# Low halves of the last weight tiles moved from VectorE to GpSimd, and three gathered-row dots a lot instead of one, in the routing stage of a hybrid block

## The chip, the cores and the metric

One Trainium2 chip, one core. The metric is device time in microseconds (us) of one execution of the whole program, the median of several runs. Three runs of the kernel before took 2127.27, 2131.42 and 2134.3 us.

## The reference, cut to what matters

A streaming encoder block: projection, sparse attention and a linear recurrence, a gated join with layer norm, and then PEER, a retrieval of single-neuron experts. The change lies in PEER alone. `eb` is the expert chosen (128 picks a token), `gb` its gate:

```python
def _peer(x, wq, subkeys, u, v):
    q = (xf @ wq).reshape(n, PEER_HEADS, 2, PEER_HALF)
    s = jnp.einsum('nhpd,hpkd->nhpk', q, subkeys)
    s_top, i_top = lax.top_k(s, PEER_TOPK)                 # 16 of 128, two sides
    cand = s_top[:, :, 0, :, None] + s_top[:, :, 1, None, :]
    best_s, best_j = lax.top_k(cand.reshape(n, PEER_HEADS, -1), PEER_TOPK)
    ...
    h = jnp.einsum('nd,nhkd->nhk', xb, u[eb])              # one dot a pick
    coef = gb * jax.nn.gelu(h, approximate=False)
    return jnp.einsum('nhk,nhkd->nd', coef, v[eb])
```

There are 16384 experts of width 1024 and 512 tokens. All of it is float32.

## The kernel before, in words

The program runs in stages, with a barrier of all engines between them: projection, attention, scan, join, then `route` (L1536) and `experts` (L1974).

**Two ways to reach the experts.** Tokens 128 to 511 (384 of them) are done densely: every expert's hidden value is computed and multiplied by a gate that is zero for experts not picked. Tokens 0 to 127 are done by gathering: GpSimd (POOL) issues an indirect DMA (`gather_rows`, L1944) that brings one picked row of `u`, later of `v`, for each of the 128 tokens, 512 KB at a time, into one of 8 slots. VectorE takes the dot of the rows with the tokens (`dot_rows`, L1956, one custom instruction over 128x1024 and a short read of the accumulator) or adds the scaled rows to the sum (`add_rows`, L1965). There are 128 dots and then 128 adds. The first `GATHERED_EARLY` = 24 dots are done in `route`, the rest in `experts`.

**float32 products.** A product is made of three passes: high by high, low part of the tokens by high of the weight, and low of the weight by high of the tokens. ScalarE (ACT) copies a weight tile of 128x1024 to its high part (`high`, L1660, `w_hl[..., 0, :]`), and another engine subtracts it from the staged tile, which gives the low part (`low`). TensorE does 16 matmuls with the high part (L1739), waits for the low part, and does 8 more (L1743).

**The route stage.** A stream of weight tiles passes through a ring of four (SP loads, ACT makes the high part, somebody the low part, TensorE multiplies). 56 tiles come first (six a head, and 8 in between), and their low parts are made by GpSimd (L1640) while VectorE ranks the scores (L1822 to L1886). Then come 24 *lots* (`LOTS`). A lot makes the dense gates of 16 tokens, from one-hot matrices, and has two tiles of the stream (2 x 24 = 48):

- VectorE: `four` (L1912) four times a lot. Each makes the one-hot matrices of four tokens by two comparisons of 128x512 (L1918, L1920) and one product of 128x1024 (L1922). Before the first lot, in the middle of each and at the end of each but the last, it makes the low part of a tile (`low`, L1926 to L1929, 48 in all), and after each lot one dot of a gathered row (L1941).
- TensorE: tile, two fours (L1796), tile, two fours.
- ACT: the high parts, the gelu of each tile's product, its store ("parked"), and the copies of the fours' sums to the lot (L1712).
- SP: the load of tile s + 4 once the low part of s is made, and the store of the lot.
- POOL: after the 56 low parts it issues the 24 gathers. From the ninth on each waits until its slot has been used.

VectorE may run four fours ahead of TensorE (L1917), no more. `RING` is also 4, so the high part of a tile waits for the product four tiles before it.

**The experts stage.** 128 steps k. For each, `v` tile k is loaded, split in high (ACT) and low (VectorE, L2179), the hidden values are weighed with the gates (L2170) and split (L2085, L2174), and TensorE adds 18 matmuls of 512 columns (L2135). The hidden values of the first 88 (`PARKED`) come from DRAM; the last 40 are computed here (L2121, L2125), with the low part of their `u` tile by VectorE (L2158). A table `used_by` says how many gathered rows VectorE has taken by the end of each step: one a step in the first 88, and the rest spread evenly over the 37 after them:

```python
used_by = [GATHERED_EARLY + (k + 1 if k < PARKED else
           min(PARKED + (2 * PICKS - GATHERED_EARLY - PARKED) * (k + 1 - PARKED) // (FRESH - 3),
               2 * PICKS - GATHERED_EARLY))
           for k in range(EXPERT_KEYS)]
```

After the last step come the layer norm and the stores.

Of the kernel before, what the change touches and what calls it, by code (L numbers as in the profile page):

```python
# [18 lines left out]
F32 = mybir.dt.float32  # L19
# [3 lines left out]
ALU = mybir.AluOpType  # L23
# [23 lines left out]
LOTS = DENSE // LOT  # L47
BETWEEN = 8
PARKED = 4 * PEER_HEADS + BETWEEN + 2 * LOTS
GATHER_RING, GATHERED_EARLY = 8, 24  # L50
MARK, FILL, LOW = -3.4e38, -3.3e38, -1.0e30


# [1482 lines left out]
def route(nc, a, g):  # L1536

    ps, ident, h1T, h_hl, dense, parked = g["ps"], g["ident"], g["h1T"], g["h_hl"], g["dense"], g["parked"]
    h_tok, gathering = g["h_tok"], g["gathering"]
# [4 lines left out]
    TILES_A_LOT = 2  # L1544
# [6 lines left out]
    RING = 4  # L1551
    with ExitStack() as ctx:
# [33 lines left out]
        rows_landed, rows_order = sem("rows_landed"), sem("rows_order")  # L1586
        landed = [sem(f"w_landed{j}") for j in range(RING)]
        h_high, h_low = sem("h_high"), sem("h_low")
        w_high, w_low, late_low = sem("w_high"), sem("w_low"), sem("late_low")
        tile_done, gelu_made = sem("tile_done"), sem("gelu_made")  # L1590
        act_parked = [sem(f"act_parked{j}") for j in range(2)]
        keys_landed, counted = sem("sub_keys_landed"), sem("counted")
# [5 lines left out]
        hot_ready, four_done, four_copied = sem("hot_ready"), sem("four_done"), sem("four_copied")  # L1598
        lot_stored = [sem(f"lot_stored{j}") for j in range(2)]
        block = ctx.enter_context(nc.Block())  # L1600
        BY_POOL = FIRST_LOT
        tile_bank = lambda n, is_query: n % 2 if is_query else 2 + n % 2

        def expert_of(s):
# [3 lines left out]
        @block.sync  # L1608
        def _(sp):
            def load(s, j):  # L1610
                sp.dma_start(staged[:, j % RING, :], a["stream"][s]).then_inc(landed[j % RING], 16)

            for j in range(RING):
                load(j, j)
            sp.dma_start(g_row, a["ln1_g"].partition_broadcast(P)).then_inc(rows_landed, 16)
            sp.dma_start(b_row, a["ln1_b"].partition_broadcast(P)).then_inc(rows_landed, 16)
            sp.dma_start(sub_keys[:, :, :], a["sub_keys"]).then_inc(keys_landed, 16)
            with sp.Fori(0, BY_POOL // 8) as i:
                for j in range(8):
                    sp.wait_ge(w_low, i * 8 + (j + 1))  # L1620
                    load(i * 8 + (j + RING), j)
            for n in range(LOTS):
                for s in range(FIRST_LOT + TILES_A_LOT * n, FIRST_LOT + TILES_A_LOT * (n + 1)):
                    if s + RING < STREAMED:
                        sp.wait_ge(late_low, s - BY_POOL + 1)
                        load(s + RING, s)
                sp.wait_ge(four_copied, 4 * (n + 1))
                sp.dma_start(dense[n], lot[:, n % 2, :, :].rearrange("p k n -> p (k n)")).then_inc(lot_stored[n % 2], 16)
            for j in range(2):
                sp.wait_ge(lot_stored[j], 16 * (LOTS // 2))  # L1630
                sp.wait_ge(act_parked[j], 16 * (PARKED // 2 + 1))

        @block.gpsimd
        def _(pool):
            nc.gpsimd.iota(count16[:, :], [[1, K]], 0, 0, allow_small_or_imprecise_dtypes=True).then_inc(counted, 1)
            nc.gpsimd.iota(count128[:, :], [[1, P]], 0, 0, allow_small_or_imprecise_dtypes=True).then_inc(counted, 1)

            def low(s, j):
                pool.wait_ge(w_high, s + 1)
                nc.gpsimd.tensor_tensor(w_hl[:, j % RING, 1, :], staged[:, j % RING, :],  # L1640
                                        w_hl[:, j % RING, 0, :].bitcast(F32), ALU.subtract).then_inc(w_low, 1)

            with pool.Fori(0, BY_POOL // 8) as i:
                for j in range(8):
                    low(i * 8 + j, j)
            pool.wait_ge(gathering["picked"], 1)
            for n in range(GATHERED_EARLY):
                gather_rows(nc, pool, a, gathering, n)

        @block.scalar  # L1650
        def _(act):
# [75 lines left out]
        @block.tensor  # L1727
        def _(pe):
            pe.sem_inc(tile_done, 1)

            def tile(s, j, m, is_query, before, low):

                pe.wait_ge(w_high, s + 1)
                pe.wait_ge(*before)
                lo, hi = (0, SEQ) if is_query else (SEQ - DENSE, SEQ)
                bank = ps[:, tile_bank(m, is_query), 0:hi - lo]
                for k in range(KD):
                    for part in range(2):
                        nc.tensor.matmul(bank, w_hl[:, j % RING, 0, P * k:P * (k + 1)], h_hl[:, part, k, lo:hi],  # L1739
                                         start=(k == 0 and part == 0), stop=False)  # L1740
                pe.wait_ge(*low)
                for k in range(KD):
                    last = nc.tensor.matmul(bank, w_hl[:, j % RING, 1, P * k:P * (k + 1)], h_hl[:, 0, k, lo:hi],  # L1743
                                            start=False, stop=(k == KD - 1))
                last.then_inc(tile_done, 1)

            def scores(i, r):
                pe.wait_ge(keys_landed, 16)
                for x in range(2):
                    pe.wait_ge(q_copied, i * 4 + (2 * r + x + 3))  # L1750
                    pe.wait_ge(s_copied, i * 4 + (2 * r + x + 1))
                    for t in range(NT):
                        last = nc.tensor.matmul(ps[:, 4 + 2 * r + x, P * t:P * (t + 1)], qT[:, x, P * t:P * (t + 1)],
                                                sub_keys[:, i * 4 + (2 * r + x), :], start=True, stop=True)
                    last.then_inc(s_done, 1)

            pe.wait_ge(h_high, KD)
            pe.wait_ge(h_low, KD)

            with pe.Fori(0, PEER_HEADS // 2) as i:  # L1760
                for j in range(2 * PER_HEAD):
                    r, m = j // PER_HEAD, j % PER_HEAD
                    s = i * (2 * PER_HEAD) + j
                    if m < 2:
                        tile(s, j, m, True, (q_copied, i * 4 + (2 * r + m + 1)), (w_low, s + 1))
                        continue
                    if m == 3:
                        scores(i, r)
                    n = 4 * r + m - 2
                    tile(s, j, n, False, (gelu_made, i * 8 + (n + 1)), (w_low, s + 1))  # L1770

            def expert(s):
                n = expert_of(s)
                tile(s, s, n, False, (gelu_made, n + 1),
                     (w_low, s + 1) if s < BY_POOL else (late_low, s - BY_POOL + 1))

            for j in range(BETWEEN):
                if j == GATES_AT:
                    pe.wait_ge(s_copied, QUERIES + 4)
                    pe.wait_ge(gates_ready, 1)  # L1780
                    for x in range(3):
                        for t in range(1, NT):
                            last = nc.tensor.transpose(ps[:, 4 + x, P * (t - 1):P * t], picks[:, x, t, :], ident[:, :])
                        last.then_inc(picks_turned, 1)
                expert(TOPK_TILES + j)
            pe.wait_ge(picks_copied, 3)

            def four(u):

                q = u % 4  # L1790
                if u >= 4:
                    pe.wait_ge(four_copied, u - 3)
                pe.wait_ge(hot_ready, u + 1)
                for n in range(FOUR):
                    for part in range(2):
                        last = nc.tensor.matmul(ps[:, 4 + q, P * n:P * (n + 1)], hot2[:, q, n, :],  # L1796
                                                hot1_hl[:, q, part, n, :], start=(part == 0), stop=(part == 1))
                last.then_inc(four_done, 1)

            for n in range(LOTS):  # L1800
                for half in range(2):
                    expert(FIRST_LOT + TILES_A_LOT * n + half)
                    four(4 * n + 2 * half)
                    four(4 * n + 2 * half + 1)

        @block.vector
        def _(dve):
# [115 lines left out]
                                 gate_hl[:, :, now].bitcast(F32).unsqueeze(3).broadcast_to([P, 2, FOUR, P]), ALU.mult  # L1923
                                 ).then_inc(hot_ready, 1)

            def low(s):  # L1926
                dve.wait_ge(w_high, s + 1)
                v_.tensor_tensor(w_hl[:, s % RING, 1, :], staged[:, s % RING, :],  # L1928
                                 w_hl[:, s % RING, 0, :].bitcast(F32), ALU.subtract).then_inc(late_low, 1)  # L1929

            low(BY_POOL)
            for n in range(LOTS):
                four(4 * n)
                four(4 * n + 1)
                low(BY_POOL + TILES_A_LOT * n + 1)
                four(4 * n + 2)
                four(4 * n + 3)
                if n + 1 < LOTS:
                    low(BY_POOL + TILES_A_LOT * (n + 1))
                if n < GATHERED_EARLY:  # L1940
                    dot_rows(nc, dve, h_tok, gathering, n)  # L1941


def gather_rows(nc, pool, a, gathering, n):  # L1944
# [347 lines left out]
```

## Time and profile before

| | before |
|---|---|
| median of 3 runs | 2131.42 us |
| lowest, highest | 2127.27, 2134.3 us |
| the profiled execution, its own time | 2135.26 us |
| its span in the trace | 2133.5 us |
| TensorE / VectorE / ACT / GpSimd busy | 1929.4 / 1608.0 / 757.5 / 567.8 us |
| route, from its first instruction to the last lot's store | 758.3 to 1379.5 us |
| of it the 24 lots on VectorE | 1071.4 to 1378.1 us |
| experts | 1384.5 us to the end |

In the rows below PE is TensorE, PEld its weight loads, DVE VectorE, ACT ScalarE, POOL GpSimd, SP SyncE; a trailing q is an engine's queue. A row of a group of instructions gives busy time, mean of one, and the idle time before it. DVE instructions overlap a little at their ends, so that the step from one start to the next (for instance 1.14 us) is shorter than the duration written (1.22 us). Idle time of an engine that is not the bottleneck costs nothing.

### The profile page before, as it was taken

Reading aid. Unit: us, or ns where it says so; the run is one execution under the profiler, and the core shown is the slowest. Engines: PE = TensorE matmul, PEld = TensorE weight load, DVE = VectorE, ACT = ScalarE, POOL = GpSimd, SP = SyncE. Lnnn points to the kernel's source line nnn. Section 1 sums busy time; section 2 is a strip of 40 time slices with the busy share of each in tenths; the row PEclk is TensorE's granted clock in tenths of the full one; section 3 lists DMA queues with packets and bytes.
Section 4 is the critical chain, followed back from the end, with each engine's and each line's share of the span. In section 5 each row is a group of like instructions: output and inputs, shape, how many; then the busy total and the mean of one; then the engine's idle time right before and its main releaser. Section 6 shows DMA issues by size and latency. Waiting matters only on the chain. (4 is left out here: it accounts for less than half of the span.)

```text
span 2133.5 us, 33188 instructions
## 1 busy us (share of the span) xinstructions
PE 1929.4 (90%) x12866; PEld 1648.7 (77%) x12866; DVE 1608.0 (75%) x2830; ACT 757.5 (36%) x1114; POOL 567.8 (27%) x395
## 2 busy tenths in 40 slices
PE   5989998889998979999499999849999999999996
PEld 4878875359863469999499999738888888999995
DVE  6288993314545279999699999848888888899998
ACT  3222554432220043333145555423333333333332
POOL 2322442000000044555200000022222224566660
PEclk9989998778999989999799999969999999999998
DMA  3211231010041054444366676399999998999992
GB/s 121 79 50 60 90 118 40 1 41 3 4 159 40 0 177 128 133 135 144 110 217 234 231 242 209 146 342 343 361 355 343 362 350 305 375 388 379 380 402 107
DMA packets 169683, 410.97 MB, mean 193 GB/s; under 512 B 13504, under 2 KB 85184, under 8 KB 166352
## 3 DMA queue, kind: packets, MB, share of 16 engines
q1 hardware_dynamic: 117712, 253.41, 34.8%
q0 software_dynamic: 36864, 134.23, 16.7%
q10 hardware_dynamic: 14976, 21.50, 2.8%
q8 instruction: 92, 1.51, 0.3%
q14 instruction: 39, 0.32, 0.0%
HBM read 360.33 MB, written 48.76 MB: 192 GB/s over the span
## 5 line engine op out<-in xcount | busy, mean ns | idle before, releaser
L2135 PE MATMUL ps<-v_hl,coef_hl 128*128 128x512 f32 x2304 | 535.6, 392 | 40.1 <-DVE coef_hl L2174 40.1
L2135 PEld LDWEIGHTS ps<-v_hl,coef_hl 128*128 128x128 f32 x2304 | 434.6, 189 | 130.7 <-DVE coef_hl L2174 41.5
L1739 PE MATMUL ps<-h_hl,w_hl 128*128 128x384 f32 (+1 forms) x1664 | 329.0, 350 | 8.8 <-DVE h_hl L1811 8.8
L1739 PEld LDWEIGHTS ps<-h_hl,w_hl 128*128 128x128 f32 x1664 | 295.8, 191 | 20.1 <-issue 9.2
L1951 POOL DMA_INDIRECT gathered_rows<-in_u_rows,pick_index x128 | 134.8, 1053 | 612.6 <-DVE pick_hidden L1961 499.9
L2079 ACT ACTIVATE v_hl<-v_staged 128x1024 fp32r<-128x1024 f32 x128 | 135.3, 1057 | 260.6 <-PE ps L2135 193.4
L2179 DVE TENSOR_TENSOR v_hl<-v_staged,v_hl 128x1024 fp32r<-128x1024 f32 x128 | 156.6, 1223 | 68.8 <-ACT v_hl L2079 68.0
L1951 POOL DMA_INDIRECT gathered_rows<-in_v,pick_index x128 | 176.2, 1377 | 104.9 <-DVE h_tok L1970 74.1
L1640 POOL TENSOR_TENSOR w_hl<-w_staged,w_hl 128x1024 fp32r<-128x1024 f32 x56 | 143.1, 2558 | 152.7 <-ACT w_hl L1665 152.4
L1970 DVE SCALAR_TENSOR_TENSOR h_tok<-gathered_rows,pick_hidden,h_tok 128x1024 f32<-128x1024 f32 x128 | 164.2, 1283 | 10.1
L1743 PE MATMUL ps<-h_hl,w_hl 128*128 128x384 f32 (+1 forms) x832 | 168.0, 343 | 0.7 <-DVE w_hl L1928 0.7
L633 PE MATMUL ps<-hT_hl,w_hl 128*128 128x264 f32 (+1 forms) x1024 | 167.9, 322 | 0.0
L633 PEld LDWEIGHTS ps<-hT_hl,w_hl 128*128 128x128 f32 x1024 | 150.4, 198 | 14.4 <-issue 2.8
L298 POOL TENSOR_TENSOR w_hl<-w_staged,w_hl 128x1024 fp32r<-128x1024 f32 x40 | 102.8, 2572 | 211.9 <-ACT w_hl L481 211.9
L1961 DVE CUSTOM_DVE_ANT_0 gathered_rows<-gathered_rows,h_tok 128x1024 f32<-128x1024 f32 x128 | 155.2, 1219 | 0.0
L1743 PEld LDWEIGHTS ps<-h_hl,w_hl 128*128 128x128 f32 x832 | 147.4, 188 | 6.0 <-DVE w_hl L1928 1.0
L2085 ACT ACTIVATE coef_hl<-coef 128x384 fp32r<-128x384 f32 x128 | 65.7, 513 | 160.8 <-DVE coef L2170 160.8
L1665 ACT ACTIVATE w_hl<-w_staged 128x1024 fp32r<-128x1024 f32 x104 | 110.5, 1064 | 24.0 <-ACT h1T L1671 16.0
L2121 PE MATMUL ps<-h_hl,u_hl 128*128 128x384 f32 x640 | 118.4, 336 | 0.0
L1922 DVE TENSOR_TENSOR hot_hl<-h1T,gate_hl 128x1024 fp32r<-128x1024 f32 x96 | 117.2, 1220 | 0.0
L2121 PEld LDWEIGHTS ps<-h_hl,u_hl 128*128 128x128 f32 x640 | 113.1, 188 | 3.1
L1712 ACT ACTIVATE lot<-ps 128x512 f32<-128x512 f32 x96 | 99.7, 1099 | 35.2 <-PE ps L1796 35.0
(319 smaller groups left out, 2791.1 us busy)
## 6 DMA issues: line engine op xcount, KB each, us to landing
v_staged<-in_v SPq DMA_DIRECT2D x128, 512.0 KB
w_staged<-in_stream SPq DMA_DIRECT2D x104, 512.0 KB
dense_gates<-lot SPq DMA_DIRECT2D x24, 1024.0 KB, 4.8
gates<-dense_gates SPq DMA_DIRECT2D x16, 1536.0 KB
w_staged<-in_w_in_t SPq DMA_DIRECT2D x40, 512.0 KB
h1T<-in_stream SPq DMA_DIRECT2D x40, 512.0 KB
parked_gelu<-h1T ACTq DMA_DIRECT2D x88, 192.0 KB
coef<-parked_gelu SPq DMA_DIRECT2D x88, 192.0 KB
```

Of the source, the lines that this page charges most:

```text
L633: nc.tensor.matmul(banks[b], w_hl[:, j, 0, P * k:P * (k + 1)], hT_hl[:, part, k, lo:hi], start=(k == 0 and part == 0), stop=False)
L1640: nc.gpsimd.tensor_tensor(w_hl[:, j % RING, 1, :], staged[:, j % RING, :], w_hl[:, j % RING, 0, :].bitcast(F32), ALU.subtract).then_inc(w_ ...
L1739: nc.tensor.matmul(bank, w_hl[:, j % RING, 0, P * k:P * (k + 1)], h_hl[:, part, k, lo:hi], start=(k == 0 and part == 0), stop=False)
L1743: last = nc.tensor.matmul(bank, w_hl[:, j % RING, 1, P * k:P * (k + 1)], h_hl[:, 0, k, lo:hi], start=False, stop=(k == KD - 1))
L1922: v_.tensor_tensor(hot1_hl[:, r], is_key[:, u % 2].unsqueeze(1).broadcast_to([P, 2, FOUR, P]), gate_hl[:, :, now].bitcast(F32).unsqueeze(3 ...
L1951: nc.gpsimd.indirect_dma_start(gathering["rows"][:, slot, :], None, table, bass.IndirectOffsetOnAxis(gathering["index"][:, column:column + ...
L1961: nc.vector.tensor_tensor_reduce(rows, rows, h_tok[:, 0, :], 1.0, 0.0, ALU.mult, ALU.add, gathering["hidden"][:, n:n + 1]).then_inc(gather ...
L1970: nc.vector.scalar_tensor_tensor(h_tok[:, 0, :], gathering["rows"][:, slot, :], gathering["hidden"][:, pick:pick + 1], h_tok[:, 0, :], ALU ...
L2079: nc.scalar.activation(v_hl[:, k % HLS, 0, :], v_staged[:, k % STAGED, :], ACT.Copy).then_inc(v_high, 1)
L2121: nc.tensor.matmul(bank, u_hl[:, f % 2, 0, P * c:P * (c + 1)], h_hl[:, part, c, SEQ - DENSE:SEQ], start=(c == 0 and part == 0), stop=False)
L2135: last = nc.tensor.matmul(ps[:, 2 + 2 * t + half, :], coef_hl[:, k % HLS, c, P * t:P * (t + 1)], v_hl[:, k % HLS, v, 512 * half:512 * (hal ...
L2179: v_.tensor_tensor(v_hl[:, k % HLS, 1, :], v_staged[:, k % STAGED, :], v_hl[:, k % HLS, 0, :].bitcast(F32), ALU.subtract).then_inc(v_low, 1)
```

## The change

GpSimd makes the low parts of all 104 tiles of the route stage, in its own order of work: after the 56 it issues six gathers, and then for each lot it makes two low parts and issues up to three gathers. VectorE makes none. It does three dots a lot instead of one, one in the middle and two after the fours. `GATHERED_EARLY` goes from 24 to 72, which also changes `used_by`. One semaphore counts all low parts.

```diff
--- before.py
+++ after.py
@@ -47,7 +47,8 @@
 LOTS = DENSE // LOT
 BETWEEN = 8
 PARKED = 4 * PEER_HEADS + BETWEEN + 2 * LOTS
-GATHER_RING, GATHERED_EARLY = 8, 24
+GATHER_RING, DOTS_A_LOT = 8, 3
+GATHERED_EARLY = DOTS_A_LOT * LOTS
 MARK, FILL, LOW = -3.4e38, -3.3e38, -1.0e30
 
 
@@ -1586,7 +1587,7 @@
         rows_landed, rows_order = sem("rows_landed"), sem("rows_order")
         landed = [sem(f"w_landed{j}") for j in range(RING)]
         h_high, h_low = sem("h_high"), sem("h_low")
-        w_high, w_low, late_low = sem("w_high"), sem("w_low"), sem("late_low")
+        w_high, w_low = sem("w_high"), sem("w_low")
         tile_done, gelu_made = sem("tile_done"), sem("gelu_made")
         act_parked = [sem(f"act_parked{j}") for j in range(2)]
         keys_landed, counted = sem("sub_keys_landed"), sem("counted")
@@ -1598,7 +1599,6 @@
         hot_ready, four_done, four_copied = sem("hot_ready"), sem("four_done"), sem("four_copied")
         lot_stored = [sem(f"lot_stored{j}") for j in range(2)]
         block = ctx.enter_context(nc.Block())
-        BY_POOL = FIRST_LOT
         tile_bank = lambda n, is_query: n % 2 if is_query else 2 + n % 2
 
         def expert_of(s):
@@ -1615,14 +1615,14 @@
             sp.dma_start(g_row, a["ln1_g"].partition_broadcast(P)).then_inc(rows_landed, 16)
             sp.dma_start(b_row, a["ln1_b"].partition_broadcast(P)).then_inc(rows_landed, 16)
             sp.dma_start(sub_keys[:, :, :], a["sub_keys"]).then_inc(keys_landed, 16)
-            with sp.Fori(0, BY_POOL // 8) as i:
+            with sp.Fori(0, FIRST_LOT // 8) as i:
                 for j in range(8):
                     sp.wait_ge(w_low, i * 8 + (j + 1))
                     load(i * 8 + (j + RING), j)
             for n in range(LOTS):
                 for s in range(FIRST_LOT + TILES_A_LOT * n, FIRST_LOT + TILES_A_LOT * (n + 1)):
                     if s + RING < STREAMED:
-                        sp.wait_ge(late_low, s - BY_POOL + 1)
+                        sp.wait_ge(w_low, s + 1)
                         load(s + RING, s)
                 sp.wait_ge(four_copied, 4 * (n + 1))
                 sp.dma_start(dense[n], lot[:, n % 2, :, :].rearrange("p k n -> p (k n)")).then_inc(lot_stored[n % 2], 16)
@@ -1640,12 +1640,17 @@
                 nc.gpsimd.tensor_tensor(w_hl[:, j % RING, 1, :], staged[:, j % RING, :],
                                         w_hl[:, j % RING, 0, :].bitcast(F32), ALU.subtract).then_inc(w_low, 1)
 
-            with pool.Fori(0, BY_POOL // 8) as i:
+            with pool.Fori(0, FIRST_LOT // 8) as i:
                 for j in range(8):
                     low(i * 8 + j, j)
             pool.wait_ge(gathering["picked"], 1)
-            for n in range(GATHERED_EARLY):
+            for n in range(2 * DOTS_A_LOT):
                 gather_rows(nc, pool, a, gathering, n)
+            for n in range(LOTS):
+                for s in range(FIRST_LOT + TILES_A_LOT * n, FIRST_LOT + TILES_A_LOT * (n + 1)):
+                    low(s, s)
+                for x in range(DOTS_A_LOT * (n + 2), min(DOTS_A_LOT * (n + 3), GATHERED_EARLY)):
+                    gather_rows(nc, pool, a, gathering, x)
 
         @block.scalar
         def _(act):
@@ -1771,8 +1776,7 @@
 
             def expert(s):
                 n = expert_of(s)
-                tile(s, s, n, False, (gelu_made, n + 1),
-                     (w_low, s + 1) if s < BY_POOL else (late_low, s - BY_POOL + 1))
+                tile(s, s, n, False, (gelu_made, n + 1), (w_low, s + 1))
 
             for j in range(BETWEEN):
                 if j == GATES_AT:
@@ -1923,22 +1927,14 @@
                                  gate_hl[:, :, now].bitcast(F32).unsqueeze(3).broadcast_to([P, 2, FOUR, P]), ALU.mult
                                  ).then_inc(hot_ready, 1)
 
-            def low(s):
-                dve.wait_ge(w_high, s + 1)
-                v_.tensor_tensor(w_hl[:, s % RING, 1, :], staged[:, s % RING, :],
-                                 w_hl[:, s % RING, 0, :].bitcast(F32), ALU.subtract).then_inc(late_low, 1)
-
-            low(BY_POOL)
             for n in range(LOTS):
                 four(4 * n)
                 four(4 * n + 1)
-                low(BY_POOL + TILES_A_LOT * n + 1)
+                dot_rows(nc, dve, h_tok, gathering, DOTS_A_LOT * n)
                 four(4 * n + 2)
                 four(4 * n + 3)
-                if n + 1 < LOTS:
-                    low(BY_POOL + TILES_A_LOT * (n + 1))
-                if n < GATHERED_EARLY:
-                    dot_rows(nc, dve, h_tok, gathering, n)
+                for x in range(DOTS_A_LOT * n + 1, DOTS_A_LOT * (n + 1)):
+                    dot_rows(nc, dve, h_tok, gathering, x)
 
 
 def gather_rows(nc, pool, a, gathering, n):
```

## Rows read from the trace of the kernel before

**Rows 1.** The page: busy time of the engines, and the span in 40 slices
```profile
PE 1929.4 (90%) x12866; PEld 1648.7 (77%) x12866; DVE 1608.0 (75%) x2830; ACT 757.5 (36%) x1114; POOL 567.8 (27%) x395
...
DVE  6288993314545279999699999848888888899998
```

**Rows 2.** Busy time by stretch: lots, parked steps, fresh steps, two stretches of other stages
```profile
core 0: us, PE busy (x) PEld busy (x) DVE busy (x) ACT busy (x) POOL busy (x), PEclk, DMA share, GB/s
1072.00:1377.00 305.00, 289.11 (x1894) 286.41 (x1895) 305.00 (x383) 160.98 (x186) 18.33 (x16) 0.99 0.62 213
1440.00:1760.00 320.00, 320.00 (x1413) 265.05 (x1413) 259.44 (x392) 115.70 (x158) 79.26 (x79) 1.00 1.00 352
1774.00:2097.00 323.00, 323.00 (x1635) 294.09 (x1635) 299.92 (x310) 107.55 (x152) 189.37 (x137) 1.00 0.96 359
684.00:701.20 17.20, 11.87 (x25) 4.94 (x24) 5.80 (x3) 0.00 (x0) 0.00 (x0) 0.80 0.00 0
460.40:477.60 17.20, 13.16 (x249) 10.59 (x248) 5.49 (x28) 5.62 (x17) 0.00 (x0) 0.68 0.35 126
```

**Rows 3.** Instructions in order of time, one lot and the start of the next
```profile
1200.29 0.68 DVE L1918 TENSOR_TENSOR h1T<-count,picksT 128x512 f32<-128x512 f32 x1
1200.63 1.15 POOL L1951 DMA_INDIRECT gathered_rows<-in_u_rows,pick_index  x1 [11.63 <-DVE pick_hidden L1961]
...
1201.49 1.22 DVE L1922 TENSOR_TENSOR hot_hl<-h1T,gate_hl 128x1024 fp32r<-128x1024 f32 x1
...
1202.63 0.68 DVE L1918 TENSOR_TENSOR h1T<-count,picksT 128x512 f32<-128x512 f32 x1
...
1211.92 1.22 DVE L1961 CUSTOM_DVE_ANT_0 gathered_rows<-gathered_rows,h_tok 128x1024 f32<-128x1024 f32 x1
...
1213.06 0.69 DVE L1918 TENSOR_TENSOR h1T<-count,picksT 128x512 f32<-128x512 f32 x1
```

**Rows 4.** Groups of instructions (busy, mean ns, idle before), the lots (1072 to 1377 us)
```profile
L1928 DVE TENSOR_TENSOR w_hl<-w_staged,w_hl 128x1024 fp32r<-128x1024 f32 x48 | 58.6, 1220 | 0.0
```

**Rows 5.** Instructions in order of time, VectorE's first work in the lots and its last four
```profile
1071.39 1.23 DVE L1928 TENSOR_TENSOR w_hl<-w_staged,w_hl 128x1024 fp32r<-128x1024 f32 x1
...
1375.72 1.23 DVE L1922 TENSOR_TENSOR hot_hl<-h1T,gate_hl 128x1024 fp32r<-128x1024 f32 x1
```

**Rows 6.** Lines L1818 (VectorE) and L1640 (GpSimd): duration ns min/median/max, first and last start
```profile
L1818 DVE TENSOR_TENSOR h_tok<-h_tok,gathered_rows x8: 1212/2306/3419, 768.8 to 785.7; 128x1024 f32<-128x1024 f32 x8
...
L1640 POOL TENSOR_TENSOR w_hl<-w_staged,w_hl x56: 2339/2402/3384, 764.0 to 1052.1; 128x1024 fp32r<-128x1024 f32 x56
```

**Rows 7.** Instructions in order of time, where GpSimd's low parts meet VectorE's work
```profile
1004.06 4.55 DVE L1873 TENSOR_TENSOR is_place<-place,count 128x1024 f32<-128x1024 f32 x2
...
1005.04 2.49 POOL L1640 TENSOR_TENSOR w_hl<-w_staged,w_hl 128x1024 fp32r<-128x1024 f32 x1 [1.84 <-ACT w_hl L1665]
...
1044.02 0.69 DVE L1894 TENSOR_TENSOR picks<-picks,small 128x512 f32<-128x512 f32 x1
...
1046.40 2.34 POOL L1640 TENSOR_TENSOR w_hl<-w_staged,w_hl 128x1024 fp32r<-128x1024 f32 x1 [34.26 <-ACT w_hl L1665]
...
1046.52 2.77 DVE L1900 TENSOR_TENSOR picks<-picks,small 128x512 f32<-128x512 f32 x1
```

**Rows 8.** GpSimd before the lots: its first and its third gather
```profile
1054.61 1.12 POOL L1951 DMA_INDIRECT gathered_rows<-in_u_rows,pick_index  x1 [0.17 <-issue]
...
1057.28 0.94 POOL L1951 DMA_INDIRECT gathered_rows<-in_u_rows,pick_index  x1 [0.30 <-issue]
```

**Rows 9.** First products of the first and of the last fresh step on TensorE
```profile
1773.47 0.87 PE L2121 MATMUL ps<-h_hl,u_hl 128*128 128x384 f32 x4
...
2097.43 0.87 PE L2121 MATMUL ps<-h_hl,u_hl 128*128 128x384 f32 x4
```

**Rows 10.** Instructions in order of time after the last fresh product
```profile
2103.05 1.23 PEld L2135 LDWEIGHTS ps<-v_hl,coef_hl 128*128 128x128 f32 x6 [0.32 <-DVE coef_hl L2174]
...
2105.12 9.43 PEld L2135 LDWEIGHTS ps<-v_hl,coef_hl 128*128 128x128 f32 x42 [0.84 <-DVE coef_hl L2174]
```

## The prediction

> **What bounds the kernel now.** I read the busy line and the slices first. TensorE is busy for 90% of the span, and VectorE stands at 9 tenths in slices 21 to 25, which are the lots [rows 1]. The share of the whole says little here, so I took one stretch of each part that the change touches [rows 2]. In the lots VectorE is busy 305.00 us of 305.00 and TensorE 289.11: VectorE is the bound, and TensorE is close behind. In the parked and the fresh steps of the experts stage TensorE is busy 320.00 of 320.00 and 323.00 of 323.00, and VectorE has room (259.44 and 299.92). So what VectorE does in the lots is on the path that sets the end, and what it does in the experts stage is beside it.
>
> In order of time a lot reads as follows [rows 3]. A four goes from 1200.29 (two comparisons) over 1201.49 (its product) to the next four at 1202.63, which is 1.20 + 1.14 = 2.34 us. The dot steps from 1211.92 to the next comparison at 1213.06: 1.14 us. The low part is of the same size; its mean duration is 1220 ns [rows 4], against 1.22 of the dot, and I take the same 1.14 us step. The lot is then 4 x 2.34 + 2 x 1.14 + 1.14 = 12.78 us, and the rows say 1213.06 - 1200.29 = 12.77. VectorE has no gap at all.
>
> **The change, part by part.** VectorE's own work first. Two low parts a lot (2.28 us) go and two dots (2.28 us) come: nothing, lot for lot. At the two ends something is left. From the first low part at 1071.39 to the end of the last product of a four, 1375.72 + 1.23 = 1376.95 [rows 5], VectorE did 96 fours, 48 low parts and 23 dots (the last dot comes after). Now it does 96 fours and 70 dots (three in each of 23 lots and one in the last; two follow the last four). 71 instructions become 70: -1.1 us. So by count alone the lots gain a microsecond. The 48 dots taken from the experts stage are the only gain left, and there they are beside TensorE.
>
> How much that is worth: the first product of the first fresh step is at 1773.47, that of the last at 2097.43, and there are 39 steps between [rows 9]. 323.96 / 39 = 8.31 us a step, with TensorE full all the way. Fewer rows a step (96 over 37 steps, 2.6, in place of 144, 3.9) free VectorE, not TensorE: 0. In the parked steps there is one row a step before and after, so they stay as they are. The gelu and the change from dots to adds move from a fresh to a parked step; VectorE has 60 us of room over 320 there, and three buffers stand between it and TensorE: 0, and up to 3 us if the buffers do not cover it. At the very end TensorE waits for VectorE's last low parts of the coefficients, 0.32 + 0.84 us [rows 10]. A VectorE that is not behind takes these away: -1.2 us, between 0 and -2.
>
> **Now what GpSimd brings.** Its low part takes 2339 to 3384 ns, median 2402 [rows 6], twice VectorE's. Two of these and three issues of gathers at about 1.15 us [rows 3] are 2 x 2.40 + 3 x 1.15 = 8.3 us of a lot of 12.78, so GpSimd has the time. The question is what VectorE does meanwhile. Line L1818 is a product or sum of two tiles in SBUF, 128x1024 on VectorE, as the low part is. It takes 1212 ns at least and 3419 ns at most, within 17 us in which GpSimd makes low parts [rows 6]. The excess is 3419 - 1212 = 2.21 us, about the duration of one GpSimd low part. GpSimd's own longest is longer by about 1 us, a VectorE instruction. The two take turns. It holds for operands that are repeated, as those of the comparisons are: two of L1873 take 4.55 us with one GpSimd low part begun 0.98 us into them [rows 7], against 2 x 1.14 + 0.08 = 2.36 without, so 2.19 us more. It holds for 128x512: L1900 takes 2.77 us with GpSimd's 1046.40 beside it, L1894 of the same shape 0.69 [rows 7], so 2.08 us more. In the lots before, GpSimd only issued gathers, and nothing of this was to be seen.
>
> The Trainium skill says the same in other words, and it speaks against the change: by "SBUF — State Buffer", section "Who interferes with whom", a VectorE instruction with two inputs in SBUF and a GpSimd instruction that reads SBUF share an interface, and the second to issue is blocked until the first is done. By that rule alone the dots would be held up as well, which no row of before shows; the trace agrees with it for products, sums and comparisons.
>
> Where the low parts of the lots fall. After the 56 low parts GpSimd's first gather starts at 1054.61 and its third at 1057.28 [rows 8], 1.34 us for each; six of them and two low parts end at about 1054.6 + 8.0 + 4.8 = 1067.4, before VectorE's lots begin at 1071.39 [rows 5]. These two cost nothing. From then on the third gather of a lot waits for the dot in the middle of the lot before it, because of the ring of eight, and the two low parts of the next lot stand behind that gather on GpSimd's queue. They begin some 1.6 us after the middle dot (0.3 to the issue, 1.15 for it), so both meet the third and fourth four, whose nine or so microseconds are all comparisons and products; no dot and no gap covers them. They end some 5 us before TensorE's next tile asks for them, and SP's loads, which wait for the low parts, leave no later than before. So 46 low parts (48 less 2) hold VectorE for their time: 46 x 2.2 = 101 us. Bounds: 46 x 2.08 = 96 (L1900) and 46 x 2.40 = 110 (the whole median of GpSimd's instruction). I take 2.2, from L1818, since its row is a steady stream as the lots are.
>
> Sum: -1.1 + 101 + 0 - 1.2 = +99 us (92 to 112). A lot goes from 12.8 to 17.2 us. TensorE's need is 289.11 / 24 = 12.0 us a lot, so it waits some 5 us in each. DMA: two more gathers of 512 KB a lot, but 4.4 us more time for them; at 213 GB/s before [rows 2] that is about 3.7 MB in 17.2 us, much the same rate.
>
> **The profiled execution** took 2135.26 us, 3.8 above the median 2131.42. 2135.3 + 99 = 2234, and on the scale of the median 2131.4 + 99 = 2230.
>
> **The rivals.**
>
> *TensorE's clock makes it the bound.* With 5 us of idle in 17.2, most of it in one gap before the fourth four, the granted clock may fall. Stretches of this length with TensorE busy 11.87 and 13.16 us were granted 0.80 and 0.68 [rows 2]. TensorE becomes the bound below 12.0 / 17.2 = 0.70. Against it: an engine that is late has no gaps, and in the lots of before, with hardly any gap, it was 0.99. If it takes 18.3 us a lot: 24 x 1.1 = 26 more, 2256.
>
> *Part of the low parts is covered.* If the pieces of a four with repeated operands let GpSimd in, or GpSimd slides under the dots at the end of the lot (2.3 us of the 4.4) and these do not take turns with it, up to half is saved: -50, 2180; with a quarter, 2205. Against: L1873, and the place in the order worked out above.
>
> *No turns are taken in the lots* (the other side: not slower). Place: the comparisons and products of L1918 to L1922 against L1640. If these forms do not meet GpSimd, nothing of the 101 us remains and -1.1 - 1.2 gives 2129. It decides as soon as a low part costs VectorE less than 2.3 / 46 = 0.05 us. For it speaks only that these very lines were never seen beside a GpSimd low part. This is also the case in which the change does nothing at all.
>
> **How the numbers follow.** Turns are taken at full price: 0.80, 2230, its own range 2222 to 2243. TensorE's clock: 0.07. Partly covered: 0.07. Not slower: 0.06. The range reaches from a quarter covered to the case of the clock, 2203 to 2256. A measurement of this kernel can tell about 0.3% (6.4 us) from no change. Faster by more than that needs a gain that I can't find in any row: 0.01. The same: 0.05. Slower: 0.94.
>
> **What would show it.** Right: the three lines of a four with maxima 2.2 us above their present 0.69 and 1.22, in pairs in the third and fourth four of a lot; their sum of busy time higher by some 100 us; GpSimd's low parts at 2.4 to 3.4 us; a lot of 17.2 us, with TensorE idle in it by some 5 us, put down to hot_hl; fresh steps still at 8.31 us. Wrong: a lot of 12.8 us (no turns), or one of over 18 us with TensorE full at a lower clock, or dots longer than 1.22 us, which would say that the low parts lie elsewhere than I put them.

## The result and the profile after

The changed kernel takes 2244.11 us, the median of 4 runs (2242.41 to 2253.25), against 2131.32 before (4 runs too): a ratio of 1.0539, interval 1.0506 to 1.0573, or 113 us more. The profiled execution took 2244.01 us over a span of 2242.3.

The page, with the same lines as [rows 1], and the busy time by stretch that answers to the first three stretches of [rows 2] (lots, parked steps, fresh steps):

```profile
PE 1977.2 (88%) x12866; PEld 1692.8 (75%) x12866; DVE 1669.0 (74%) x2782; ACT 759.1 (34%) x1114; POOL 682.6 (30%) x443
...
DVE  5388973134452599996999999956888877778776
```
```profile
1072.00:1480.00 408.00, 332.32 (x1842) 322.52 (x1842) 408.00 (x415) 159.65 (x182) 189.68 (x110) 0.87 0.60 218
1555.00:1875.00 320.00, 320.00 (x1413) 264.96 (x1413) 259.75 (x364) 115.99 (x157) 84.80 (x78) 1.00 1.00 352
1884.00:2206.00 322.00, 322.00 (x1629) 293.11 (x1629) 251.02 (x251) 108.25 (x155) 120.35 (x89) 1.00 0.82 283
```

VectorE is busy throughout the lots, as before (408.00 of 408.00 us), but they are 114 us longer. In the fresh steps it has 71 us of room where it had 23, and TensorE is full there as before: the dots moved out of that stage bought nothing.

VectorE's groups in the lots, 1072 to 1480 us (busy, mean ns, idle before), and below them the instructions of VectorE and GpSimd in order of time in half a lot:

```profile
L1926 DVE TENSOR_TENSOR hot_hl<-h1T,gate_hl 128x1024 fp32r<-128x1024 f32 x92 | 223.0, 2424 | 0.0
L1957 DVE CUSTOM_DVE_ANT_0 gathered_rows<-gathered_rows,h_tok 128x1024 f32<-128x1024 f32 x70 | 83.4, 1215 | 0.0
L1922 DVE TENSOR_TENSOR h1T<-count,picksT 128x512 f32<-128x512 f32 x92 | 64.8, 705 | 0.0
L1924 DVE TENSOR_TENSOR hot<-count,picksT 128x512 fp32r<-128x512 f32 x92 | 62.6, 680 | 0.0
```
```profile
1214.95 0.68 DVE L1922 TENSOR_TENSOR h1T<-count,picksT 128x512 f32<-128x512 f32 x1
...
1215.55 0.68 DVE L1924 TENSOR_TENSOR hot<-count,picksT 128x512 fp32r<-128x512 f32 x1
...
1216.15 6.15 DVE L1926 TENSOR_TENSOR hot_hl<-h1T,gate_hl 128x1024 fp32r<-128x1024 f32 x1
1216.46 4.75 POOL L1640 TENSOR_TENSOR w_hl<-w_staged,w_hl 128x1024 fp32r<-128x1024 f32 x2
```

The product of a four has a mean of 2424 ns; before, the lines of a four had no instruction over 1.23 us [rows 3, 5]. The excess is not spread over them. One product a lot, the first behind the middle dot, takes 6.15 us, and inside it lie both of GpSimd's low parts. 21 of the 96 products are like this (mean 6131 ns), one took 8414 with three low parts inside, and all others 1.2 us. In the whole stage L1922 had one at 2881 ns. No dot was held.

From the first comparison of the lots to the end of the last product it is 304.4 us before and 418.5 after: +114.0. The rest of the 108.8 us between the two spans is small: the stages ahead of `route`, which the change does not touch, ended 4.4 us earlier in this execution; the low part ahead of the first four is gone (-1.0); up to the first sum -0.1; the parked steps +0.7; the 40 fresh steps 0.0; the end -0.3. From the first comparison to the end of the span it is 1061.0 us before and 1175.2 after, 114.2 more, so nothing behind the lots gave any of it back.

### The profile page after: what moved, and what is told of

The parts are those of the page before. It is cut to its first block and busy times, and to the rows that moved or that the text cites. A ratio compares the mean times of both kernels' runs of the same rounds, so it can differ in the third digit from the quotient of the medians.

```text
span 2242.3 us, 33187 instructions
## 1 busy us (share of the span) xinstructions
PE 1977.2 (88%) x12866; PEld 1692.8 (75%) x12866; DVE 1669.0 (74%) x2782; ACT 759.1 (34%) x1114; POOL 682.6 (30%) x443
## 5 line engine op out<-in xcount | busy, mean ns | idle before, releaser
L1744 PE MATMUL ps<-h_hl,w_hl 128*128 128x384 f32 (+1 forms) x1664 | 359.5, 373 | 8.7 <-DVE h_hl L1815 8.7
L1744 PEld LDWEIGHTS ps<-h_hl,w_hl 128*128 128x128 f32 x1664 | 326.8, 210 | 20.1 <-issue 9.1
L1640 POOL TENSOR_TENSOR w_hl<-w_staged,w_hl 128x1024 fp32r<-128x1024 f32 x104 | 256.8, 2483 | 160.9 <-ACT w_hl L1670 160.1
L1947 POOL DMA_INDIRECT gathered_rows<-in_u_rows,pick_index x128 | 144.1, 1126 | 404.7 <-DVE pick_hidden L1957 364.8
L1947 POOL DMA_INDIRECT gathered_rows<-in_v,pick_index x128 | 168.0, 1312 | 282.6 <-DVE h_tok L1966 241.0
L1926 DVE TENSOR_TENSOR hot_hl<-h1T,gate_hl 128x1024 fp32r<-128x1024 f32 x96 | 227.9, 2374 | 0.0
L1800 PE MATMUL ps<-hot_hl,hot 128*128 128x128 f32 x768 | 114.1, 302 | 77.4 <-DVE hot_hl L1926 77.4
L1800 PEld LDWEIGHTS ps<-hot_hl,hot 128*128 128x128 f32 x768 | 107.8, 217 | 87.7 <-issue 60.4
L1748 PE MATMUL ps<-h_hl,w_hl 128*128 128x384 f32 (+1 forms) x832 | 168.0, 343 | 0.0
L299 POOL TENSOR_TENSOR w_hl<-w_staged,w_hl 128x1024 fp32r<-128x1024 f32 x40 | 102.9, 2572 | 211.8 <-ACT w_hl L482 211.8
L1748 PEld LDWEIGHTS ps<-h_hl,w_hl 128*128 128x128 f32 x832 | 147.9, 188 | 5.0
L1717 ACT ACTIVATE lot<-ps 128x512 f32<-128x512 f32 x96 | 99.7, 1081 | 117.0 <-PE ps L1800 117.0
L2166 DVE TENSOR_TENSOR coef<-coef,gates 128x384 f32<-128x384 f32 x128 | 71.1, 555 | 78.1 <-ACT coef L2086 56.2
## 6 DMA issues: line engine op xcount, KB each, us to landing
gates<-dense_gates SPq DMA_DIRECT2D x16, 1536.0 KB, 13.8
```

The costliest lines, as they stand in the source:

```text
L1926: v_.tensor_tensor(hot1_hl[:, r], is_key[:, u % 2].unsqueeze(1).broadcast_to([P, 2, FOUR, P]), gate_hl[:, :, now].bitcast(F32).unsqueeze(3 ...
L1947: nc.gpsimd.indirect_dma_start(gathering["rows"][:, slot, :], None, table, bass.IndirectOffsetOnAxis(gathering["index"][:, column:column + ...
```

## The experiments

Each time is a median of two to ten runs, set against the kernel before, run again at the same time (2127.9 to 2129.4 us). The ratios are those on record over all runs and can differ from the quotient of the two medians in the fourth digit. "The lots" is the stretch from the first comparison to the end of the last product, in the profiled execution. The price of a low part is what the lots take above VectorE's own count, divided by 46. The count is 2.341 us for each of the 96 fours and 1.144 us for each dot ahead of the last product, which are the steps where nothing meets them.

**Only the low parts moved.**

```diff
-GATHER_RING, DOTS_A_LOT = 8, 3
+GATHER_RING, DOTS_A_LOT = 8, 1
```

> The changed kernel with one dot a lot instead of three: of the change only the low parts are moved. Theory (GpSimd and VectorE take turns at their SBUF inputs): VectorE's own work is 12.8 - 2.3 = 10.5 us a lot, and the two low parts of GpSimd hold it for 2 x 2.2 to 2 x 2.45 us more, as in the changed kernel, where 21 products took 6.13 us in place of 1.22. A lot is 14.9 to 15.4 us, the lots from the first comparison to the last product 304 + 23 x (2.1 to 2.6) = 353 to 364 us, the whole 2180 to 2192 us. Rival (the two further gathers of a lot are what costs, through GpSimd's queue or the DMA engines): VectorE is free of low parts and TensorE is the bound with 12.0 us a lot, and the whole is 2115 to 2125 us.

2177.5 us against 2128.8 (ratio 1.0231, 1.0197 to 1.0264): a little below the band of the theory, and far from the rival. The lots took 350.8 us. VectorE's count is 96 x 2.341 + 23 x 1.144 = 251.0, so 99.7 / 46 = 2.17 us a low part. Three dots are among the instructions held (3.39 to 3.40 us). VectorE and GpSimd here, in order of time:

```profile
1204.64 1.21 DVE L1926 TENSOR_TENSOR hot_hl<-h1T,gate_hl 128x1024 fp32r<-128x1024 f32 x1
1205.77 1.21 DVE L1957 CUSTOM_DVE_ANT_0 gathered_rows<-gathered_rows,h_tok 128x1024 f32<-128x1024 f32 x1
...
1206.91 2.86 DVE L1922 TENSOR_TENSOR h1T<-count,picksT 128x512 f32<-128x512 f32 x1
```
```profile
1204.44 4.79 POOL L1640 TENSOR_TENSOR w_hl<-w_staged,w_hl 128x1024 fp32r<-128x1024 f32 x1 [5.56 <-ACT w_hl L1670]
```

GpSimd's low part starts at 1204.44, within a comparison, and lets a product and a dot pass that began after it; then the next comparison is held, 2.86 us in place of 0.68. 11 of the 46 low parts were passed in this way. The low parts come as ScalarE's high parts come, one at a time, and what VectorE has next is held.

**Only the dots moved.** The kernel before, with the low parts by VectorE:

```diff
-GATHER_RING, GATHERED_EARLY = 8, 24
+GATHER_RING, DOTS_A_LOT = 8, 3
+GATHERED_EARLY = DOTS_A_LOT * LOTS
...
                 low(BY_POOL + TILES_A_LOT * n + 1)
+                dot_rows(nc, dve, h_tok, gathering, DOTS_A_LOT * n)
...
-                if n < GATHERED_EARLY:
-                    dot_rows(nc, dve, h_tok, gathering, n)
+                for x in range(DOTS_A_LOT * n + 1, DOTS_A_LOT * (n + 1)):
+                    dot_rows(nc, dve, h_tok, gathering, x)
```

> The kernel before with three dots a lot and 72 early gathers, the low parts still made by VectorE: of the change only the dots are moved. Theory: nothing but their count costs, 47 dots before the last product x 1.14 = 54 us more in the lots (15.1 us a lot), the product at 1.22 us throughout, and nothing back in the experts stage, whose fresh steps stay at 8.31 us: 2131 + 54 = 2185 us, 2181 to 2190. Rival (taking gathers out of the experts stage frees something there): a few to 10 us less than that, with fresh steps under 8.31 us. With the run that moves only the low parts, the two should add up to the 113 us of the change.

2178.6 us (1.0236, 1.0203 to 1.0269), 50 us more in the median and 2 us below the band. The lots took 358.7, which is 54.3 more, as counted (47 x 1.144 = 53.8), with no instruction of VectorE over 1.25 us in them. From the first comparison to the end of the span it is 1115.0 us against 1061.0, so the 54 us are there in full; what is missing lies ahead of the lots, where the edit changes nothing (the first comparison is at 1061.5 here and at 1072.5 before). The fresh steps stayed at 8.31 us: from 1816.69 to 2140.65 over 39. So nothing came back, and the rival is out. Low parts alone (+46.4 in the lots) and dots alone (+54.3) make 100.7 of the 114.0. The 13.3 that are left are in the price of a low part: 2.17 us with the low parts alone, (418.5 - 304.8) / 46 = 2.47 in the changed kernel, and 46 x 0.30 = 13.8.

**Does the dot take turns as well?** The three dots together in the middle, and the low parts released by the first of them:

```diff
+            for s in range(FIRST_LOT, FIRST_LOT + TILES_A_LOT):
+                low(s, s)
             for n in range(LOTS):
-                for s in range(FIRST_LOT + TILES_A_LOT * n, FIRST_LOT + TILES_A_LOT * (n + 1)):
+                pool.wait_ge(gathering["used"], DOTS_A_LOT * n + 1)
+                for s in range(FIRST_LOT + TILES_A_LOT * (n + 1), min(FIRST_LOT + TILES_A_LOT * (n + 2), STREAMED)):
+                    low(s, s)
...
-                dot_rows(nc, dve, h_tok, gathering, DOTS_A_LOT * n)
+                for x in range(DOTS_A_LOT * n, DOTS_A_LOT * (n + 1)):
+                    dot_rows(nc, dve, h_tok, gathering, x)
                 four(4 * n + 2)
                 four(4 * n + 3)
-                for x in range(DOTS_A_LOT * n + 1, DOTS_A_LOT * (n + 1)):
-                    dot_rows(nc, dve, h_tok, gathering, x)
```

> The changed kernel with the three dots of a lot together in its middle, and GpSimd's two low parts of the next lot released by the first of them, ahead of its gathers, so that the low parts begin some 0.3 us into the second dot. Theory A (the dot, a custom instruction with two SBUF inputs, takes turns too): a dot of about 6 us in place of the long product, a lot stays at 17.7 us and the whole at 2235 to 2250 us. Theory B (the dot does not meet GpSimd): dots stay at 1.22 us, some 2 us of each lot's 4.8 us of low parts run beneath them, the instruction after them is held for the rest (about 3 us), a lot is 15.5 to 16.2 us and the whole 2190 to 2210 us.

2232.7 us (1.0490, 1.0457 to 1.0524), 2 us below the range of theory A and 23 above that of theory B. In order of time:

```profile
1207.81 1.22 DVE L1959 CUSTOM_DVE_ANT_0 gathered_rows<-gathered_rows,h_tok 128x1024 f32<-128x1024 f32 x1
1207.96 6.62 POOL L1640 TENSOR_TENSOR w_hl<-w_staged,w_hl 128x1024 fp32r<-128x1024 f32 x2 [6.22 <-DVE pick_hidden L1959]
...
1208.95 3.38 DVE L1959 CUSTOM_DVE_ANT_0 gathered_rows<-gathered_rows,h_tok 128x1024 f32<-128x1024 f32 x1
...
1212.26 2.87 DVE L1925 TENSOR_TENSOR h1T<-count,picksT 128x512 f32<-128x512 f32 x1
```

The dot is held too: 23 dots have a mean of 3396 ns. Theory B is out. But theory A's six-microsecond dot is not there either. The engines alternate: GpSimd waits for the dot that runs (two low parts take 6.62 us in place of 4.75), the next dot waits for GpSimd, the second low part for that dot, the comparison for the second low part. The price is (408.5 - 307.1) / 46 = 2.20 us. The Trainium skill's "SBUF — State Buffer", section "Who interferes with whom", says that a VectorE instruction with two inputs in SBUF contends with a GpSimd instruction that reads SBUF. The dot has two such inputs, and at 3396 ns in place of 1218 the trace agrees.

**One input out of SBUF.** The same work as the changed kernel, with the counting row and the gates copied once to two free banks of PSUM:

```diff
...
+            count_ps, gate_ps = ps[:, 0, DENSE:DENSE + P], ps[:, 0:2, 0:DENSE]
+            v_.tensor_copy(count_ps, count128[:, :]).then_inc(in_psum, 1)
+            v_.tensor_copy(gate_ps, gate_hl[:, :, :].bitcast(F32)).then_inc(in_psum, 1)
+            dve.wait_ge(in_psum, 2)
...
-                count = count128[:, :].unsqueeze(1).broadcast_to([P, FOUR, P])
+                count = count_ps.unsqueeze(1).broadcast_to([P, FOUR, P])
...
-                                 gate_hl[:, :, now].bitcast(F32).unsqueeze(3).broadcast_to([P, 2, FOUR, P]), ALU.mult
+                                 gate_ps[:, :, now].unsqueeze(3).broadcast_to([P, 2, FOUR, P]), ALU.mult
```

> The changed kernel with one operand of each instruction of a four in PSUM (the counting row for both comparisons, the gates for the product, in two banks that are free by then): same work, one SBUF input instead of two. Theory (it is the second SBUF input that meets GpSimd's reads): the products stay near 1.22 us or what an operand in PSUM makes of them, GpSimd's low parts take 2.34 to 2.4 us, a lot is 12.8 us and the whole 2126 to 2135 us. If PSUM makes an instruction slower by 0.1 us, 12 x 24 x 0.1 = 29 us more. Rival (any VectorE instruction, or its writes, meets GpSimd): 2240 to 2250 us as before.

2163.4 us (1.0164, 1.0133 to 1.0195): 81 us less than the changed kernel, and 28 above the upper end of what the theory gave. Lines of the product and of the dot (duration ns min/median/max), and a piece in order of time:

```profile
L1930 DVE TENSOR_TENSOR hot_hl<-h1T,ps x96: 1201/1206/1219, 1071.7 to 1405.4; 128x1024 fp32r<-128x1024 f32 x96
```
```profile
L1961 DVE CUSTOM_DVE_ANT_0 gathered_rows<-gathered_rows,h_tok x128: 1207/1218/4833, 1075.2 to 1672.5; 128x1024 f32<-128x1024 f32 x128
```
```profile
1203.76 4.74 POOL L1640 TENSOR_TENSOR w_hl<-w_staged,w_hl 128x1024 fp32r<-128x1024 f32 x2
```
```profile
1205.98 1.21 DVE L1930 TENSOR_TENSOR hot_hl<-h1T,ps 128x1024 fp32r<-128x1024 f32 x1
1207.11 2.49 DVE L1961 CUSTOM_DVE_ANT_0 gathered_rows<-gathered_rows,h_tok 128x1024 f32<-128x1024 f32 x1
```

44 products in which a low part began took 1207 ns. Their output is in SBUF as before, so it is the second input that meets GpSimd, not the write. What is left is the dots, whose inputs are still both in SBUF: the low parts end at 1208.50, the fours at 1207.11, so 21 dots stand at about 2.5 us, one at 3.4 and one at 4.8. All 72 took 119.9 us instead of 87.5, which is 32 us. A slower operand in PSUM, which the expectation had priced at 29 us, would have given nearly the same total, but no instruction of a four was slower: the longest product took 1219 ns, the longest comparison 693.

**The dot out of the low parts' way.** The same with the middle dot ahead of all four fours of a lot:

```diff
+                dot_rows(nc, dve, h_tok, gathering, DOTS_A_LOT * n)
                 four(4 * n)
                 four(4 * n + 1)
-                dot_rows(nc, dve, h_tok, gathering, DOTS_A_LOT * n)
```

> The run with one operand of the fours in PSUM and three dots a lot took 34 us more than the kernel before, and in it 22 dots of 72 stood at 2.5 us: the low parts began 1.3 us after the middle dot and ran 4.8 us, past the two fours that follow (4.7 us), into a dot. Here the middle dot stands ahead of all four fours, so that the low parts have 9.3 us of fours to run beside. Theory (only the dots meet GpSimd now): no dot over 1.3 us, lots 305 us, the whole 2126 to 2134 us, the same as before the change, with three dots a lot and all low parts made by GpSimd. Rival (something else of the three dots costs, such as 295 GB/s of loads in the lots): 2150 to 2165 us.

2126.9 us (0.9999, 0.9985 to 1.0013): no difference from before. The dot's line now says

```profile
L1961 DVE CUSTOM_DVE_ANT_0 gathered_rows<-gathered_rows,h_tok x128: 1212/1216/1225, 1063.1 to 1632.2; 128x1024 f32<-128x1024 f32 x128
```

and the lots took 302.5 us, with the same two more gathers a lot. With the meetings gone, the change costs nothing, and gains nothing, as its count of instructions said. The rival is out.

**The operand in PSUM by itself,** in the kernel before (same edit):

> The kernel before, with nothing changed but one operand of each instruction of a four in PSUM. In the last run the product took 1206 ns in place of 1219 and the comparisons 0.68 us as ever. So the operand in PSUM is worth nothing by itself: 2126 to 2134 us, no difference that can be told. If it were worth more (over 6 us), the gain of the run with one dot would not be GpSimd's.

2130.7 us against 2129.4 (1.0001, 0.9982 to 1.0021): no difference that can be told.

**One input in PSUM and one dot a lot,** the low parts by GpSimd: the edit with PSUM above, and `DOTS_A_LOT` from 3 to 1:

> As the run with one operand of each instruction of a four in PSUM, but with one dot a lot, as before the change: GpSimd makes the low parts, VectorE has only the fours (which no longer meet them) and one dot. Theory: VectorE needs 4 x 2.34 + 1.14 = 10.5 us a lot, and at most one dot a lot is held, by 1.3 to 2.2 us; TensorE needs 12.0 us a lot and becomes the bound, so that the lots last about 24 x 12.1 = 290 us against 304 before, and the whole takes 2113 to 2122 us. Rival (the lots stay bound by something else, such as ScalarE's copies or the loads behind the low parts): 2127 to 2135 us, no gain.

2113.8 us against 2129.4 (0.9917, 0.9892 to 0.9942), 16 us or 0.8% faster than before, within the band of the theory. The lots took 280.6 us against 304.4. Busy time by stretch in the lots:

```profile
1072.00:1355.00 283.00, 281.78 (x1874) 281.64 (x1874) 276.14 (x332) 158.40 (x184) 124.29 (x64) 0.99 0.67 235
```

TensorE is full with 281.78 of 283.00. VectorE leads it by a few fours. Its dots are still held in 21 cases (2.5 us); with TensorE full beside them that should cost nothing now, but no run has this kernel without the held dots. VectorE's last product ends at 1349.5 and the last lot's store goes 9.1 us later, where it was 2.5 before, so some of the 24 us are given back.

**Is it the pairing that costs 0.3 us more?** The two low parts of a lot apart on GpSimd's queue, each behind one gather:

```diff
...
                 low(s, s)
+                if n >= 1:
+                    pool.wait_ge(gathering["used"], DOTS_A_LOT * n - 1)
+                for x in xs[:1]:
+                    gather_rows(nc, pool, a, gathering, x)
                 low(s + 1, s + 1)
+                for x in xs[1:]:
+                    gather_rows(nc, pool, a, gathering, x)
```

> The changed kernel with the two low parts of a lot apart on GpSimd's queue: the first behind the gather that waits for the middle dot, the second behind the next gather, which waits for a dot at the end of the lot. In the changed kernel both lie within one product, GpSimd goes twice without VectorE getting a turn between, and a low part costs 113.6 / 46 = 2.47 us; in the two runs where they met VectorE one at a time (only the low parts moved, and under the dots) it was 99.7 / 46 = 2.17 and 101.4 / 46 = 2.20. Theory A (it is the pairing that costs the 0.27 us more): 2.2 us each, the lots 406 us from the first comparison to the last product, the whole 2229 to 2237 us. Theory B (a low part that meets a product costs 2.4 us or more either way): the lots 414 to 420 us, the whole 2239 to 2250 us.

2247.4 us (1.0547, 1.0504 to 1.0590), as theory B had it. Pairing is not the cause; the lots took 422.6 us, 2.56 us a low part, even more. GpSimd, then VectorE:

```profile
1215.50 2.40 POOL L1640 TENSOR_TENSOR w_hl<-w_staged,w_hl 128x1024 fp32r<-128x1024 f32 x1
```
```profile
1215.19 3.80 DVE L1931 TENSOR_TENSOR hot_hl<-h1T,gate_hl 128x1024 fp32r<-128x1024 f32 x1
```

The product begins 0.31 us before the low part and yet waits for all of it: 0.31 + 2.40 + 1.09 = 3.80. GpSimd does not wait (2.40 is its undisturbed time), and the product's first 0.31 us seem to be lost.

**Half a low part.** The low part of the lots over 512 of 1024 columns; the other half is left out.

```diff
...
-                    low(s, s)
+                    half_low(s, s)
```

> The changed kernel with GpSimd's low parts of the lots cut to their first 512 of 1024 columns; the other half of those low parts is left out. Theory (VectorE is held for as long as GpSimd's instruction lasts): GpSimd's low part takes about 1.3 us, the held product 1.22 + 2 x 1.3 to 1.4 = 3.8 to 4.0 us, a low part costs about 1.3 us in place of 2.47, the lots 365 to 370 us in place of 418, the whole 2188 to 2200 us. Rival (a fixed price for each meeting of the two): less than 15 us gained, 2230 us or more.

2188.8 us (1.0285, 1.0259 to 1.0311). GpSimd's 46 instructions have a mean of 1306 ns in place of 2398, the 21 long products 3944 in place of 6131, and the price is (368.2 - 304.8) / 46 = 1.38 us in place of 2.47. In this order of work the hold lasts as long as GpSimd's instruction, plus about 0.07 us (1.38 against 1.31, 2.47 against 2.40). That is 0.15 us for a hold with two low parts in it; with one in each it was about the same again (2.56 against 2.40), so the run with the low parts apart pays it twice as often. The larger fixed price of the rival is not there.

## Why the prediction was right, and what was off

**VectorE is the bound of the lots, and its own work does not change** (12.8 us a lot either way, -1.1 us over all). Right: the run with all meetings removed has lots of 302.5 us against 304.4 and equals the kernel before.

**GpSimd's low parts hold VectorE.** Right in kind, shown from both sides: the hold of a four goes when one of its inputs leaves SBUF, and shrinks with GpSimd's instruction. That it holds for repeated operands, read from L1873 [rows 7], is right too.

**46 x 2.2 = 101 us** is the term that was mis-sized. It measured 46 x 2.47 = 114. The row it rests on, L1818 [rows 6], shows engines that alternate, where GpSimd starts its waiting while VectorE works. The runs in which they alternate confirm 2.2 (2.17 and 2.20). In the changed kernel they do not alternate: GpSimd's low parts come right behind a gather, begin 0.31 us into a product, take no wait themselves (2.40 us each), and the product does all its work afterwards: 0.31 + 4.75 + 1.09 = 6.15. My upper bound, 46 x 2.40 = 110, was the better model and still a little short. The whole of the 12.4 us between 46 x 2.47 and 46 x 2.2 is this. Why GpSimd goes first in one order of work and not in the other stays open (last section).

**Where they fall.** The prediction said 1.6 us behind the middle dot, in the third and fourth four. They begin 1.5 us behind it (1214.95 to 1216.46), but both are inside the product of the third four, and the fourth is undisturbed. So the sign that the prediction named, all three lines of a four with maxima 2.2 us higher and in both fours, did not come in that form: L1926 reached 8414 ns, L1922 was long once and L1924 never (at most 689 ns). That no dot would cover them was right. The rival with part of them covered by dots has also lost its ground: dots are held like the rest.

**The experts stage gives nothing.** Right: fresh steps of 8.31 us before and after, (2206.55 - 1882.59) / 39. The -1.2 us at the end came out at -0.3, and the parked steps took 0.7 more, within the 3 allowed.

**TensorE's clock.** The granted clock in the lots was 0.87, with 76 us in 408 in which TensorE was not busy. That is above the 0.70 at which it would have become the bound, so VectorE stayed it. The rival did not come. TensorE waited for `hot_hl` for 76.9 us in the lots, 3.2 us a lot and not 5: at the lower clock its own work filled part of the gap (332.32 us busy in place of 289.11).

**The sum.** +99 forecast, +113 in the medians, +108.8 in the spans; in the latter the earlier stages, which happened to be 4.4 us shorter, hide a part. 2244 lies in the range of 2203 to 2256, one microsecond above the likeliest case's own range (2222 to 2243).

## What to carry to other kernels

Work moved from a busy VectorE to an idle GpSimd is free only where the two do not meet at SBUF, that is, where VectorE's instructions have at most one input there: here an elementwise instruction of 2.4 us on GpSimd took 2.2 to 2.6 us of VectorE's time, twice the 1.14 us that VectorE needed for the same work. Look in the trace of the kernel before for instructions of one line whose longest is far above their shortest, and see whether the other engine runs within them. If one input of VectorE's instructions fits in a free bank of PSUM, or the instructions that cannot be changed are placed away from GpSimd's, the meetings cost nothing. What the move then gains is what VectorE no longer has to do, up to the next bound: nothing with three dots a lot, 16 us with one, where TensorE is the next bound.

## What the runs showed of the hardware that was not expected

An instruction of VectorE that began 0.31 us before GpSimd's did not keep its place: products of 6.13 us (21 of them, all within 6.10 to 6.17) and 3.79 us, with GpSimd at its undisturbed 2.40. In the run under the dots, where GpSimd began 0.15 us into a dot, the dot kept its place and GpSimd waited. The Trainium skill's page "SBUF — State Buffer" ("Who interferes with whom") says that the order of issue decides who is blocked, and, of VectorE's modes with two ports, that whoever issues first has the shared ports for the whole instruction. By the starts in the trace the second case agrees, the first does not, and the measurement decides. Nor do the 11 low parts agree that a product and a dot passed when the low parts alone were moved. In all cases of the first kind the low part followed directly on a gather on GpSimd's queue (the gather ends at 1216.44, the low part starts at 1216.46). This holds without exception: in the changed kernel, with the low parts apart and with half low parts, 87 low parts began within 0.02 us of the end of a gather while VectorE was at work, and each went first. In the same runs and in the two where the engines alternate, 72 began after an idle wait of GpSimd, and each let the instruction of VectorE that ran finish. Whether the gather is the cause was not tried by itself.

In the changed kernel GpSimd also went twice, and once three times (8.41 us), while the product waited, although in other runs the two alternated. What decides it stays open too. The price is 2.17 to 2.20 us a low part where GpSimd waits for VectorE, and 2.47 to 2.56 where it does not.
